# Two up loops and a gate loop: VectorE adds a pair's halves ahead of the first low-weight conversion instead of behind it

## The reference, cut to what matters

```python
def squared_relu_mlp(h, w_up, w_down):        # layers 0 and 1, w_up: 1024 x 4096
    u = jax.nn.relu(h @ w_up)
    return (u * u) @ w_down
...
# third layer, w_gate and w_up: 1024 x 2816
        h = rmsnorm(x, ffn_pre_norm[i])
        f = (jax.nn.silu(h @ w_gate[i]) * (h @ w_up[i])) @ w_down[i]
        x = x + rmsnorm(f, ffn_post_norm[i])
        e = rmsnorm(p[i] @ w_ple_proj[i], ple_norm[i])
        x = x + jax.nn.sigmoid(x @ w_ple_gate[i]) * e
```

## Time and profile before

| | |
|---|---|
| median of 3 runs | 968.42 us (968.32 to 970.42) |
| the profiled execution | 968.42 us |
| its span in the profile | 966.6 us |
| TensorE busy | 954.4 us (99%) |
| VectorE busy | 748.5 us (77%) |
| ScalarE busy | 548.3 us (57%) |
| GpSimd busy | 88.3 us (9%) |
| DMA | 172 GB/s in the mean |

### The profile page before, as it was taken

How to read it: one execution, slowest core, us unless ns; L and a number is a source line. 1 busy time by engine, 2 the same in 40 slices (tenths; PEclk the granted TensorE clock), 3 DMA queues, 4 the chain that set the end, 5 groups by cost and what they waited for, 6 DMA issues and landing times.

```text
span 966.6 us, 18482 instructions
## 1 busy us (share of the span) xinstructions
PE 954.4 (99%) x7556; PEld 911.1 (94%) x7556; DVE 748.5 (77%) x1130; ACT 548.3 (57%) x818; POOL 88.3 (9%) x91
## 2 busy tenths in 40 slices
PE   9999999999999999999999999999999999999998
PEld 8999999999999998999999999999999989999998
DVE  7898778978855599867987844489877988787777
ACT  6652366656454476655665544455566665556455
POOL 5334101000201000001000201001001000000000
PEclk9999999999999999999999999999999999999999
DMA  8743444766666836435476565626536467665651
GB/s 256 230 132 117 145 130 133 219 195 197 192 185 193 269 110 200 141 114 177 135 218 196 175 210 186 194 70 182 180 109 204 123 179 213 200 192 171 201 175 44
DMA packets 164723, 166.62 MB, mean 172 GB/s; under 512 B 6784, under 2 KB 162832, under 8 KB 164640
## 3 DMA queue, kind: packets, MB, share of 16 engines
q1 hardware_dynamic: 162752, 163.47, 55.4%
q0 software_dynamic: 1056, 1.19, 0.5%
q10 hardware_dynamic: 832, 0.79, 0.4%
HBM read 163.82 MB, written 1.08 MB: 171 GB/s over the span
## 4 chain that ended last, share of the span: by engine, by line
PE 79%; DVE 14%; issue 3%; ACT 2%; DMA 2%; SPq 0%; POOL 0%; ACTq 0%; DVEq 0%
PE ps L657 19%; PE ps L660 16%; PE ps L649 13%; DVE w_lo L1985 4%; PE ps L682 2%; PE ps L678 2%; PE ps L677 2%; PE ps L676 2%; PE ps L683 2%; PE ps L684 2%; PE ps L689 2%; PE ps L690 2%; PE ps L691 2%; DVE mo L2103 2%; DVE xs L2133 1%
## 5 line engine op out<-in xcount | busy, mean ns | idle before, releaser
L1985 DVE TENSOR_TENSOR w_lo<-w_raw,w_hi 128x1024 fp32r<-128x1024 f32 (+4 forms) x314 | 376.5, 1209 | 120.7 <-ACT w_hi L1423 115.8
L1423 ACT ACTIVATE w_hi<-w_raw 128x1024 fp32r<-128x1024 f32 x298 | 313.5, 1055 | 192.3 <-PE ps L660 39.2
L657 PE MATMUL ps<-xs,w_hi 128*128 128x256 f32 x1012 | 132.7, 277 | 0.0
L657 PEld LDWEIGHTS ps<-xs,w_hi 128*128 128x128 f32 x1012 | 127.1, 188 | 4.5
L660 PE MATMUL ps<-xs,w_lo 128*128 128x256 f32 x832 | 112.3, 277 | 0.0
L660 PEld LDWEIGHTS ps<-xs,w_lo 128*128 128x128 f32 x832 | 103.0, 188 | 0.2
L682 PE MATMUL ps<-xs,w_hi 128*128 128x256 f32 x320 | 91.5, 286 | 0.4 <-DVE w_lo L1985 0.4
L683 PE MATMUL ps<-xs,w_hi 128*128 128x256 f32 x320 | 89.3, 279 | 0.0
L684 PE MATMUL ps<-xs,w_lo 128*128 128x256 f32 x320 | 89.2, 279 | 0.0
L649 PE MATMUL ps<-xs,w_hi 128*128 128x512 f32 x326 | 85.2, 393 | 1.3 <-DVE mo L2013 0.8
L1430 ACT ACTIVATE tmp<-ps 128x512 f32<-128x512 f32 x75 | 44.4, 592 | 66.4 <-PE ps L649 57.6
(11 more groups left out here) (430 smaller groups left out, 1903.0 us busy)
## 6 DMA issues: line engine op xcount, KB each, us to landing
w_raw<-in_mlp_w_up SPq DMA_DIRECT2D x64, 512.0 KB, 4.1
w_raw<-in_mlp_w_down SPq DMA_DIRECT2D x64, 512.0 KB, 4.1
w_raw<-in_a_w_in SPq DMA_DIRECT2D x32, 512.0 KB, 4.5
w_raw<-in_w_gate SPq DMA_DIRECT2D x22, 512.0 KB, 4.0
w_raw<-in_w_up SPq DMA_DIRECT2D x22, 512.0 KB, 4.6
w_raw<-in_w_down SPq DMA_DIRECT2D x20, 512.0 KB, 4.0
w_raw<-in_w_kv SPq DMA_DIRECT2D x16, 512.0 KB, 4.0
w_raw<-in_w_in SPq DMA_DIRECT2D x16, 512.0 KB, 3.8
```

The lines of the kernel that those rows point to most:

```text
L657: mm(ps[:, 2 * pset + n, at], hi[:, kk, n * P:(n + 1) * P], x[:, kt0 + kk, at], start=False, stop=False)
L1423: o = fn(dst, raw, ACT.Copy)
L1985: return v.tensor_tensor(d, x, y, ALU.subtract)
```

## The change

In `up` and in `gu_body` the call of `lo` that stood ahead of the wait for `pair_copied` now stands behind the sum. The number of instructions, their operands and their waits stay as they were. The ScalarE and TensorE lists are not changed.

```diff
@@ up, body(i)
-                        lo(u0 + b + 2, i, 2, 0)
                         dve.wait_ge(pair_copied, c0 + b + 1 + i * 2)
                         total(pset, mo[:, 2 * b:2 * b + 2, :], slot=slot).then_inc(pair_summed, 1)
+                        lo(u0 + b + 2, i, 2, 0)
                         dve.wait_ge(pair_summed, p0 + b + 1 + i * 2)
```

## The result

| | before | changed |
|---|---|---|
| median, first comparison | 968.42 us (7 runs) | 972.11 us (970.97 to 973.24, 7 runs) |
| ratio | | 1.0036 (95%: 1.0026 to 1.0046) |
| median, second comparison (experiment 8) | 969.27 us (21 runs) | 972.11 us (971.31 to 973.39, 6 runs) |
| ratio | | 1.0030 (95%: 1.0019 to 1.0042) |
| profiled execution, its span | 968.42, 966.6 us | 972.55, 970.7 us |

The kernel became slower, by 3.7 us in the first comparison and 2.8 us in the second. The changed kernel has the same median in both. What differs are the runs of the kernel before, whose median lies between 968.4 and 969.6 us from one comparison to the next.

A forecast was written before the change was run, and what follows sets the result against it. TensorE, busy 954.4 of 966.6 us, was taken as the bound. Up loops 0, inside gate loop 0, new wait 2.58 and slower pace 0.2 gave 2.8 us on 968.42: 971.2 us, forecast range 969.9 to 972.2 (0.66).

The forecast's parts named there:

- The up loops: Both up loops: the sum is not held up by the conversion, so 0 us, bounds -0.1 and +0.3.
- The ring of the gate loop: VectorE and ScalarE waiting on each other in the gate loop: a turn takes 10.88 us instead of 10.14, TensorE's is 10.91.
- The marks of the ring: Gate loop: turn 10.88 us, even half 4.57, multiplication 2.36 after its copy, copies never bound by TensorE, last copy to rounding 4.82.
- The gap in the loop: TensorE's 0.81 us gap for a sum at 779.96, gate loop: gains and losses set to zero, bounds -0.8 and +0.5.
- The end of the loop: Behind the gate loop: last rounding 3.77 us later, less 1.19 of cover, gives 2.58 us new TensorE wait before line 816.
- The slower pace: Behind a wait, groups of eight TensorE multiplications take 1.10 us instead of 1.07: 0.2 us added, between 0 and 0.5.
- The clock: TensorE's granted clock, full in all 40 slices of the profile before: nothing charged for a fall.
- rival D: TensorE's clock falls to half rate at the new wait: up to 5.5 us more, 976.7 us; chance 0.02.
- The sum: Whole kernel: 0 + 0 + 2.58 + 0.2 = 2.8 us slower, 971.2 us.
- A: Gate loop turn shorter than 10.88 us, so a smaller lag at its end: 968.6 to 969.9 us; chance 0.17.
- B: Gate loop turn stays at 10.14 us, conversion still overlapping, so not slower at all: 967.6 us; chance 0.08.
- C: Gate loop turn of 11.1 us, above TensorE's, so the lag grows 2.0 us more: 973.2 us; chance 0.07.

The follow-up runs named there:

- experiment 8: The changed kernel again, unaltered, measured beside the kernel before: 972.11 us against 969.27, ratio 1.0030.
- experiment 1: Kernel before with the new order in the two up loops only, gate loop as before: 969.63 us against 969.55, ratio 1.0000.
- experiment 2: Kernel before with the new order in the gate loop only, up loops as before: 972.22 us against 969.55, ratio 1.0027.
- experiment 3: Kernel before with the new order only in gate loop turns 0 to 5: 970.04 us against 969.55, ratio 1.0007.
- experiment 4: Kernel before with the new order only in gate loop turns 6 to 10: 970.09 us against 969.55, ratio 1.0004.
- experiment 6: Changed kernel with VectorE's three folds of the ple squares ahead of its second conversion: 970.82 us against 969.31 for the kernel before, ratio 1.0015.

## Why the prediction was right, step by step

**The up loops, 0.** Right: experiment 1 has a ratio of 1.0000, within 0.8 us either way.

**The ring of the gate loop, 10.88 us.** Right to 0.03 us: 10.86 and, over nine turns, 10.85. The marks of the ring held: 4.56 us for the even half (4.57), the multiplication 2.35 us behind its copy (2.36), no copy bound by TensorE, and the way from the last copy to the rounding 880.28 - 875.48 = 4.80 us (4.82). The one distance that no row showed, from a sum to a conversion behind it, is 0.61 us as taken.

**The gap in the loop.** It shrank from 0.81 to 0.35 us, and a second wait of 0.38 stands at 785.47. Before there was already some 0.3 us there, hidden in a merged row (six products take 1.69 us from 785.24, 1.38 from 790.78). I had taken gain and loss as equal. Counted from the first line 816 (764.13, before 764.65), TensorE is 0.26 us later than before at 806.20 (806.46) and still 0.26 at 880.28 (880.54); in the trace of experiment 8 it is 0.05 at 883.39 (883.39 - 764.27, before 883.72 - 764.65). So this term was right to 0.3 us.

**The end of the loop, 3.77 us later, 2.58 us of new wait.** Right in kind and place. From the first steady copy to the last rounding it is 880.28 - 773.27 = 107.01 us, before 877.28 - 773.74 = 103.54: 3.47 us later, not 3.77. The missing 0.3 is nine times the 0.03 of the turn. Against it, TensorE starts line 816 at 890.23, 0.14 us after the end of the fold at 890.09, which I had not counted. 3.47 - 1.19 + 0.14 = 2.42 us. TensorE's own rows give 2.48 us between the two lines 816 (764.13 to 890.23, before 764.65 to 888.27): 0.26 inside the loop, 0.15 at a conversion of the third unit, for which TensorE waits in a merged row (1.68 us instead of 1.52 for twelve products, 885.73), and 2.07 at line 816, of which its row calls 1.91 a wait. I had forecast 2.2 to 2.6 for this row, and that sign did not hold: what TensorE had lost before is no longer lost at line 816. Experiments 2, 3 and 4 show that the lag at the end is the cause, and experiment 6 that it acts through line 816.

**The slower pace, 0.2.** Too small, and its cause is not shown. In the trace of experiment 8 eight products take 1.10 us from 891.7 to about 905. The 5.12 us from 890.59 to 895.71 were 893.48 - 888.51 = 4.97 us before, and by 910.32 it is 0.52 us in all (20.05 us behind line 816, before 907.80 - 888.27 = 19.53). That is at the upper bound of 0.5. But experiment 4 has the same stretch behind its line 816 (908.90 - 888.88 = 20.02 us), where nothing waits. So this 0.5 us can't be called a consequence of the wait.

**The clock.** I charged nothing and gave rival D 0.02, at a price of up to 5.5 us. Here the step failed in its odds: the fall happens in 4 of 13 executions of the changed kernel, and it costs 1.2 to 1.5 us when it does. The reading that I rested it on was too coarse: a 9 in the row of forty slices means 90% or more, and the page of the changed kernel also has forty of them, with the fall in it. The longest wait of the kernel before, 1.2 us at the very start, said nothing on this. The rule of the Trainium skill ("TensorE: Matmul & The Clock Gate", section "Why this matters for your kernels"), that an idle gap between bursts can send the clock back to half rate, is stated there for gaps longer than this one, a condition that I had left out when I applied it to the new wait. By it the clock should have stayed up, and in the traces of experiments 2 and 8 it did (granted clock 1.00 behind waits of 1.88 and 1.91 us). The first trace goes against it (0.50 behind a wait of 1.91 us), and there the measurement decides.

**The sum, 2.8 us.** In the trace of experiment 8, which has no fall, the change costs 2.38 us between the two lines 816 (764.27 to 890.27) and 0.52 behind them, 2.9 in all. That this meets the forecast so closely is in part luck: the end of the loop was put 0.2 too high and the slower pace 0.3 too low. So is the 2.8 us of the second comparison, since two of its six executions have a fall. The 971.2 us lies 0.9 under the first median. Without the executions with a fall the changed kernel has 971.7 us in either comparison; the rest of the first comparison's 3.7 us lies in the runs of the kernel before, 0.85 us faster there, and is not explained. The intervals of the two comparisons overlap.

**The rivals.** A (a shorter ring) happened to a tenth of its size: 0.03 us a turn. B (the conversion still overlaps) and C (the ring becomes the bound) did not happen.

## What to carry to other kernels

Where two engines pass work to and fro, add up the ring from start to start, and compare it with the bound engine's time for the same work. An instruction that stands ahead of a wait may be free, because it fills that wait; behind the wait it is in the ring. A ring that becomes only just shorter than the bound's period shows no wait inside the loop and still costs: it keeps the lag with which the loop starts, and the bill comes at the first thing behind the loop that has less cover than the lag. Here the better move was the one that shortens the ring: the sum and everything that the other engine waits for first, and both conversions last, except where the conversion is itself the next thing wanted (0.9988, 0.9979 to 0.9997).

A merged row of a timeline can hide a wait: compare its length from start to start with that of other rows of the same count.

## What the runs showed of the hardware that I had not expected

A wait of TensorE of 1.9 us, with full work before and behind, was followed by a stretch at the lower clock (granted 0.50, most of 891.3 to 894.7 us) in one trace and left it at 1.00 in two others. By the mean clock of each execution a fall came in 4 of 13 of the changed kernel and in none of the 8 of experiment 2, which has the same wait. With work of no use in the gap it came in none of 10, too few to tell that from chance.

TensorE has stretches in which 128x256 products follow each other some 4% slower (eight of them start within 0.94 instead of 0.91 us, and show 1.10 instead of 1.07) at a granted clock of 1.00. Some stand behind a wait (831 to 847 in experiment 3), some don't (890.3 to 903.8 in experiment 4, 797.4 to 801.1 in the changed kernel), and the same code can have one in one trace and not in another (173 to 188 in the kernel before, not in the changed kernel's first trace). Many last for some 15 us, which costs 0.5 to 0.6 us, as much as the differences that experiments 3 and 4 could not settle by their times. What makes them is open, and no run here was meant for it.
